# Low halves of the MLP's weights: from VectorE's subtraction to a negated copy by ScalarE and an accumulating DMA

## The chip, the cores and the metric

One core of a Trainium2 chip runs the kernel. The metric is the device time of one execution in microseconds; lower is better.

## The reference

Two layers of a hybrid decoder trunk over 512 tokens of width 1024, in float32. Each layer has a mixing part (one input projection, a gated short convolution beside chunkwise retention, one output projection) and an MLP of width 4096, each behind an RMSNorm that is modulated by a vector computed from `c`. Cut to what matters here:

```python
for l in range(DEPTH):
    mod = (c_act @ w_ada[l] + b_ada[l])[:, None, :]
    sh1, sc1, g1, sh2, sc2, g2 = jnp.split(mod, N_MOD, axis=-1)
    ...
    x = x + g1 * mix
    h2 = rms_norm(x, norm2_g[l]) * (1.0 + sc2) + sh2
    x = x + g2 * (jnp.square(jax.nn.relu(h2 @ w_up[l])) @ w_down[l])
return rms_norm(x, final_g)
```

## The kernel before

Everything is held transposed, features on partitions and the 512 tokens along the free dimension. All weights are one stream of 200 *units* of 128x1024 float32 (512 KB), 100 per layer. A unit holds eight 128x128 blocks and is the work for one bank of PSUM (or half of it, in down). There are four slots for units, `w_raw`, `w_hi` and `w_lo`, each with [4, 1024] per partition, and unit u lies in slot u % 4; four units make a *step*.

TensorE multiplies in a reduced float32 format (`F32R`), so each operand is split into a high half (the value rounded to that format) and a low half (what is left). `three` (lines 304 to 306) makes the three products high x high, high x low and low x high, so a unit is 24 matmuls. In the MLP they are 512 columns wide; a few stages around the norms are done in two halves of 256 columns.

The path of a unit in the kernel before:

- SP (`load_weight`, line 224) waits until the unit before it in the slot has been split (`w_lo_done`), and loads `w_raw` from HBM.
- ScalarE (`split_hi`, line 570) waits for the load (`w_in`) and until TensorE has finished the unit before it in the slot (`pe_unit`), and writes `w_hi` as a rounding copy.
- VectorE (`split_lo`, line 773) waits for `w_hi_done` and writes `w_lo` = `w_raw` - `w_hi`.
- TensorE (`unit`) waits for `w_lo_done` and does the 24 matmuls, then raises `pe_unit`.

`w_lo_done` is one count over all units, raised in their order; it releases TensorE and SP.

The order of work is written out by hand for each engine, in loops with semaphores. Stages of a layer, by step: v, q and k, four heads (steps up to 6), the output projection with half-width passes while the norm's statistics are made (`between` on ScalarE and VectorE), then the MLP in two halves of 2048 hidden features. Each half has *up* (16 units, one hidden tile each) and *down* (16 units, two for each of the eight output tiles). In up, each finished unit goes through four engines: ScalarE takes the relu out of PSUM to `buf_a` (line 732), GpSimd squares it into `buf_b` (line 1223), ScalarE copies the high half to `u_hi` (line 735), and VectorE subtracts for `u_lo` (line 815). `buf_a` and `buf_b` have two places each. In down, VectorE adds to `x` (`residual`, line 911), and in the second half's down ScalarE squares the new `x` and GpSimd adds the squares up (`add_square`, line 1169), once for two units.

Up's first unit-group in the first half is special (`first_step`): it goes over its four units in two half-width passes, and the second pass finishes them closely one after another, 12 half-width matmuls apart, so that the unit after them is due in slot 0 right when the fourth is finished.

VectorE also reduces the modulation's weights (`ada_pair`, line 784), 512 KB each, loaded by SP in the same queue as the units. GpSimd is otherwise idle in the MLP.

The core of a unit in the code:

```python
act.wait_ge(w_in[j], (l * STEPS + step) * 16 + 32)
act.wait_ge(pe_unit, u + 1)
nc.scalar.copy(w_hi[:, j, :], w_raw[:, j, :]).then_inc(w_hi_done, 1)
```

Of the kernel before, what the change touches and what calls it, by code (L numbers as in the profile page):

```python
# [34 lines left out]
SLOTS = 4  # L35
UNITS = 100
# [26 lines left out]

C_G1, C_G2, C_CONV, C_RET = 0, 8, 16, 28
PARAMS = 32

M_GATE1, M_SH2, M_SC2, M_GATE2 = range(2 * KT, MODS, KT)

# [2 lines left out]
ALU = mybir.AluOpType  # L71
# [4 lines left out]
def trunk(nc, xT, c_cols, weights, ada, params, bias, final_g, identity, tables, outT):  # L76
    with ExitStack() as ctx:
# [3 lines left out]
        def sem(name):  # L81
            return ctx.enter_context(nc.semaphore(name))
# [94 lines left out]
        c_exp, c_step, c_ps, c_ready = sem("c_exp"), sem("c_step"), sem("c_ps"), sem("c_ready")  # L177
        w_hi_done = sem("w_hi_done")
        w_lo_done = sem("w_lo_done")
        pe_half = sem("pe_half")  # L180
        pe_unit = sem("pe_unit")
        ada_done = sem("ada_done")
# [381 lines left out]
        def _(act):  # L564
            def split_hi(l, step, j):
# [3 lines left out]
                act.wait_ge(pe_unit, u + 1)  # L569
                nc.scalar.copy(w_hi[:, j, :], w_raw[:, j, :]).then_inc(w_hi_done, 1)  # L570

            def pe_has(l, u):
                act.wait_ge(pe_unit, l * UNITS + u + (SLOTS + 1))

# [96 lines left out]
            with act.Fori(0, DEPTH) as l:  # L671
# [55 lines left out]
                for half in range(2):  # L727

                    with act.Fori(0, 4) as i:
                        for j in range(SLOTS):  # L730
                            pe_has(l, i * 4 + (U_UP[half] + j))
                            nc.scalar.activation(buf_a[:, j % 2, :], ps[:, j, :], ACT.Relu).then_inc(evac_act, 1)  # L732
                            split_hi(l, i + (9 + 8 * half), j)
                            act.wait_ge(rsq_ready, l * 32 + i * 4 + (16 * half + j + 1))
                            nc.scalar.copy(u_hi[:, bass.ds(i * 4 + j, 1), :].rearrange("p a t -> p (a t)"),
                                           buf_b[:, j % 2, :]).then_inc(xs_hi, 1)

                    if half == 0:
                        with act.Fori(0, 4) as i:
                            for j in range(SLOTS):  # L740
                                split_hi(l, i + 13, j)

                added = l * SQ + SQ_MIX
                with act.Fori(0, 3) as i:
                    for m in range(2):
                        split_hi(l, i + 21, 2 * m)
                        act.wait_ge(evac_dve, l * ED + i * 2 + (2 + ED_DOWN[1] + m + 1))
                        act.wait_ge(ssum_added, added + i * 2 + m + 1)
                        nc.scalar.activation(buf_a[:, m, :], x[:, bass.ds(i * 2 + m, 1), :].rearrange("p a t -> p (a t)"),
                                             ACT.Square).then_inc(sq_ready, 1)  # L750
                        split_hi(l, i + 21, 2 * m + 1)

                def down_square(half, m):
                    act.wait_ge(evac_dve, l * ED + (2 + ED_DOWN[1] + 6 + half * 2 + m + 1))
# [14 lines left out]
        def _(dve):  # L769
# [83 lines left out]
            def between(l, step, xs, n, which, rest):  # L853


                def tiles(half, *ks):
                    for k in ks:
                        if k < KT:
                            product(xs, n, which, half, k)
                        if k:  # L860
                            low(xs, which, half, k - 1)
                rest(0)
                norm_scale(n, 0)
                split_lo(l, step, 0)
                tiles(0, 0, 1)
                rest(1)
                tiles(0, 2, 3, 4)
                rest(2)
                tiles(0, 5, 6)
                rest(3)  # L870
                tiles(0, 7, 8)
                dve.wait_ge(w_lo_done, l * UNITS + (step * SLOTS + 2 * SLOTS + 2))
                split_lo(l, step, 2)
                split_lo(l, step, 3)
                norm_scale(n, 1)
                tiles(1, *range(KT + 1))
# [124 lines left out]
            with dve.Fori(0, DEPTH) as l:  # L1001
# [98 lines left out]
                for half in range(2):  # L1100

                    with dve.Fori(0, 4) as i:
                        for j in range(SLOTS):
                            split_lo(l, i + (9 + 8 * half), j)
                            ub = bass.ds(i * 4 + j, 1)
                            xs_low(l, i * 4 + (XS_U[half] + j), u_lo[:, ub, :].rearrange("p a t -> p (a t)"),
                                   buf_b[:, j % 2, :], u_hi[:, ub, :].rearrange("p a t -> p (a t)"))
                            if half == 0 and j < 2:
                                ada_pair(l, i + 12, i * 2 + M_GATE2, j, later=True)
                        if half:  # L1110
                            with dve.If(l < DEPTH - 1):
                                for j in range(2):
                                    ada_pair(l, i + 20, i * 2 + KT, j, later=True)

                    if half == 0:
                        with dve.Fori(0, 4) as i:
                            for m in range(2):
                                split_lo(l, i + 13, 2 * m)
                                pe_has(l, i * 4 + (U_DOWN[0] + 2 * m + 1))
                                dve.wait_ge(mod_added, l * 24 + 24)  # L1120
                                residual(i * 2 + m, 2 + m, M_GATE2)
                                split_lo(l, i + 13, 2 * m + 1)
                            with dve.If(l < DEPTH - 1):
                                for j in range(2):
                                    ada_pair(l, i + 16, i * 2, j, later=True)
                    else:
                        with dve.Fori(0, 3) as i:
                            for m in range(2):
                                split_lo(l, i + 21, 2 * m)
                                pe_has(l, i * 4 + (U_DOWN[1] + 2 * m + 1))  # L1130
                                residual(i * 2 + m, 2 + m, M_GATE2)
                                split_lo(l, i + 21, 2 * m + 1)
                        with dve.If(l < DEPTH - 1):
                            dve.wait_ge(mod_added, l * 24 + 32)
                            norm_gain(l * 2 + 2, 0, mod[:, 1:2 * KT:2],
                                      par[:, bass.ds(below(l * PARAMS + PARAMS + C_G1, DEPTH * PARAMS, KT), KT)])

                        def down_rest(j):
                            if j % 2:
                                m = j // 2  # L1140
                                pe_has(l, U_DOWN[1] + 13 + 2 * m)
                                residual(6 + m, DOWN_BANK[1][m], M_GATE2, HALVES[1])

                        for m in range(2):
                            dve.wait_ge(pe_half, l * 6 + (SLOTS + m + 1))
                            residual(6 + m, DOWN_BANK[0][m], M_GATE2, HALVES[0])
                        with dve.If(l < DEPTH - 1):
                            between(l, 24, l * XS + XS, l * 2 + 2, 0, down_rest)
                        with dve.If(l > DEPTH - 2):
                            norm_scale(l * 2 + 2, 0)  # L1150
                            down_rest(1)
                            final(0)
                            down_rest(3)
                            norm_scale(l * 2 + 2, 1)
                            final(1)
# [3 lines left out]
        def _(pool):  # L1159
# [11 lines left out]
            def split_lo(l, step, j):  # L1171

                pool.wait_ge(w_hi_done, l * UNITS + step * SLOTS + (SLOTS + j + 1))
                nc.gpsimd.tensor_tensor(w_lo[:, j, :], w_raw[:, j, :], w_hi[:, j, :].bitcast(F32), ALU.subtract
                                        ).then_inc(w_lo_done, 1)

            pool.sem_inc(ssum_added, 2)
            pool.sem_inc(rope_done, 2)
# [7 lines left out]
            with pool.Fori(0, DEPTH) as l:  # L1186
# [31 lines left out]
                for half in range(2):  # L1218
                    with pool.Fori(0, 4) as i:
                        for j in range(SLOTS):  # L1220
                            pool.wait_ge(evac_act, l * EA + i * 4 + (EA_UP[half] + j + 1))
                            pool.wait_ge(xs_lo, l * XS + i * 4 + (XS_U[half] + j - 1))
                            nc.gpsimd.tensor_tensor(buf_b[:, j % 2, :], buf_a[:, j % 2, :], buf_a[:, j % 2, :], ALU.mult  # L1223
                                                    ).then_inc(rsq_ready, 1)

                clear_sum(l * 2 + 2)
                added = l * SQ + SQ_MIX
                with pool.Fori(0, 3) as i:
                    for m in range(2):
                        add_square(l * 2 + 2, added, i * 2 + m, m)  # L1230
                for s in range(6, SQ_MLP):
                    if s == 8:
                        with pool.If(l < DEPTH - 1):
# [89 lines left out]
```

## Time and profile before

| | |
|---|---|
| median of 3 runs | 1205.29 us (1204.19 to 1205.61) |
| span of the profiled execution | 1202.4 us; its own time was not taken apart from the runs, the median lies 2.9 us above it |
| TensorE matmul busy | 1158.5 us, 96% |
| VectorE busy | 700.7 us, 58% |
| ScalarE busy | 439.7 us, 37% |
| GpSimd busy | 274.2 us, 23% |
| DMA | 161.75 MB, 38.2% of 16 engines |

PE is TensorE's matmul side, DVE VectorE, ACT ScalarE, POOL GpSimd, SPq the queue that SP issues DMAs to. Matmuls are pipelined and their modelled spans overlap, so PE's busy share says whether it had work, not how near its peak it is. Idle time of an engine costs something only where another one waits for it.

### The profile page before, as it was taken

How to read it: one execution, taken by the hardware profiler on the slowest of the kernel's cores; microseconds unless marked ns; L12 is line 12 of the kernel's file. 1: busy time of each engine (PE TensorE's matmuls, PEld its weight loads, DVE VectorE, ACT ScalarE, POOL GpSimd, SP SyncE). 2: the span in 40 equal slices, each digit the busy share in tenths (PEclk: the TensorE clock that was granted, in tenths of full speed). 3: DMA queues.
4: the chain of work that ended last, by engine and by line, in shares of the span. 5: the costliest groups of instructions: out<-in, count | busy, mean ns of one | idle time of the engine just before them, and what ended most of it. 6: DMA issues, size and time to landing. Idle time of an engine off the chain costs nothing.

```text
span 1202.4 us, 17270 instructions
## 1 busy us (share of the span) xinstructions
PE 1158.5 (96%) x5702; PEld 978.4 (81%) x5702; DVE 700.7 (58%) x871; ACT 439.7 (37%) x620; POOL 274.2 (23%) x191
## 2 busy tenths in 40 slices
PE   2799999999999999999999999999999999999997
PEld 1688788899888888888897888889988888888886
DVE  7899877767443434443367897766764232333333
ACT  5445444335332123432243544424534212343220
POOL 4369210132110001120113940104222000112110
PEclk9899999999999999999999999999999999999998
DMA  9655434224443353343234433433353323232212
GB/s 358 259 175 179 153 108 154 101 107 160 160 141 138 105 190 125 115 147 105 87 136 158 164 140 127 138 120 123 108 192 119 105 89 103 88 105 93 98 36 72
DMA packets 46910, 161.75 MB, mean 135 GB/s; under 512 B 5520, under 2 KB 7696, under 8 KB 46736
## 3 DMA queue, kind: packets, MB, share of 16 engines
q1 hardware_dynamic: 46864, 161.13, 38.2%
q8 instruction: 29, 0.48, 0.2%
q14 instruction: 17, 0.14, 0.0%
HBM read 159.01 MB, written 2.10 MB: 134 GB/s over the span
## 4 chain that ended last, share of the span: by engine, by line
PE 80%; DVE 10%; issue 6%; POOL 2%; ACT 1%; DMA 0%; DVEq 0%; SPq 0%; ACTq 0%; POOLq 0%
PE ps L304 25%; PE ps L306 25%; PE ps L305 25%; DVE ada_raw L784 3%; DVE w_lo L773 2%; PE ps L484 1%; POOL buf_a L1202 1%; PE ps L469 1%; POOL buf_b L1203 1%; DVE arena L953 1%; PE ps L344 1%; DVE w_lo L989 1%; PE ps L345 1%; PE ps L346 1%; DVE ssum L944 0%
## 5 line engine op out<-in xcount | busy, mean ns | idle before, releaser
L773 DVE TENSOR_TENSOR w_lo<-w_raw,w_hi 128x1024 fp32r<-128x1024 f32 x193 | 259.4, 1346 | 300.8 <-ACT w_hi L570 298.7
L304 PE MATMUL ps<-h_hi,w_hi 128*128 128x512 f32 (+1 forms) x960 | 363.7, 379 | 3.4 <-issue 1.8
L306 PE MATMUL ps<-h_hi,w_lo 128*128 128x512 f32 (+1 forms) x960 | 360.9, 376 | 0.0
L305 PE MATMUL ps<-h_lo,w_hi 128*128 128x512 f32 (+1 forms) x960 | 360.7, 376 | 0.0
L570 ACT CAST w_hi<-w_raw 128x1024 fp32r<-128x1024 f32 x196 | 204.6, 1046 | 245.0 <-PE ps L306 230.7
L304 PEld LDWEIGHTS ps<-h_hi,w_hi 128*128 128x128 f32 x960 | 181.1, 189 | 37.2 <-issue 2.0
L304 PE MATMUL ps<-u_hi,w_hi 128*128 128x512 f32 (+1 forms) x576 | 211.0, 366 | 0.0
L305 PE MATMUL ps<-u_lo,w_hi 128*128 128x512 f32 (+1 forms) x576 | 210.5, 365 | 0.0
L306 PE MATMUL ps<-u_hi,w_lo 128*128 128x512 f32 (+1 forms) x576 | 210.5, 365 | 0.0
L306 PEld LDWEIGHTS ps<-h_hi,w_lo 128*128 128x128 f32 x960 | 181.0, 189 | 33.0
L305 PEld LDWEIGHTS ps<-h_lo,w_hi 128*128 128x128 f32 x960 | 181.1, 189 | 32.2
L1223 POOL TENSOR_TENSOR buf_b<-buf_a 128x512 f32<-128x512 f32 x64 | 70.6, 1103 | 450.7 <-ACT buf_a L732 447.1
L784 DVE CUSTOM_DVE_ANT_0 ada_raw<-ada_raw,c_act 128x1024 f32<-128x1024 f32 x80 | 124.4, 1568 | 2.3 <-DMA ada_raw<-ada 2.0
L305 PEld LDWEIGHTS ps<-u_lo,w_hi 128*128 128x128 f32 x576 | 108.6, 189 | 17.6
L304 PEld LDWEIGHTS ps<-u_hi,w_hi 128*128 128x128 f32 x576 | 108.6, 189 | 17.6
L306 PEld LDWEIGHTS ps<-u_hi,w_lo 128*128 128x128 f32 x576 | 108.6, 189 | 17.4
L911 DVE SCALAR_TENSOR_TENSOR x<-ps,mod,x 128x512 f32 (+2 forms) x60 | 38.5, 642 | 134.6 <-PE ps L306 134.6
L1169 POOL TENSOR_TENSOR ssum<-ssum,buf_a 128x256 f32<-128x256 f32 (+1 forms) x44 | 48.0, 1092 | 274.7 <-ACT buf_a L597 160.3
L732 ACT ACTIVATE buf_a<-ps 128x512 f32<-128x512 f32 x64 | 38.2, 597 | 160.4 <-PE ps L306 160.4
L304 PE MATMUL ps<-y_hi,w_hi 128*128 128x256 f32 (+1 forms) x192 | 61.6, 321 | 0.0
L305 PE MATMUL ps<-y_lo,w_hi 128*128 128x256 f32 (+1 forms) x192 | 61.1, 318 | 0.0
L306 PE MATMUL ps<-y_hi,w_lo 128*128 128x256 f32 (+1 forms) x192 | 61.1, 318 | 0.0
(123 smaller groups left out, 1066.7 us busy)
## 6 DMA issues: line engine op xcount, KB each, us to landing
w_raw<-weights SPq DMA_DIRECT2D x200, 512.0 KB, 3.3
ada_raw<-ada SPq DMA_DIRECT2D x80, 512.0 KB, 4.4
arena<-ada SPq DMA_DIRECT2D x16, 512.0 KB, 14.9
x<-xT SPq DMA_DIRECT2D x2, 1024.0 KB, 6.7
outT<-x SPq DMA_DIRECT2D x8, 256.0 KB, 2.3
tab<-tables SPq DMA_DIRECT2D x1, 1024.0 KB, 15.1
tab<-tables SPq DMA_DIRECT2D x1, 512.0 KB, 9.8
ident<-identity SPq DMA_DIRECT2D x1, 64.0 KB, 2.0
```

Source lines behind the costliest of these rows:

```text
L304: nc.tensor.matmul(out, wh, hi, start=first, stop=False, skip_group_check=True)
L305: nc.tensor.matmul(out, wh, lo, start=False, stop=False, skip_group_check=True)
L306: return nc.tensor.matmul(out, wl, hi, start=False, stop=last, skip_group_check=True)
L344: nc.tensor.matmul(out, hh, wh, start=start, stop=False, skip_group_check=True)
L345: nc.tensor.matmul(out, hh, wl, start=False, stop=False, skip_group_check=True)
L570: nc.scalar.copy(w_hi[:, j, :], w_raw[:, j, :]).then_inc(w_hi_done, 1)
L732: nc.scalar.activation(buf_a[:, j % 2, :], ps[:, j, :], ACT.Relu).then_inc(evac_act, 1)
L773: nc.vector.tensor_tensor(w_lo[:, j, :], w_raw[:, j, :], w_hi[:, j, :].bitcast(F32), ALU.subtract).then_inc(w_lo_done, 1)
L784: nc.vector.tensor_tensor_reduce(out=ada_raw[:, slot, :], in0=ada_raw[:, slot, :], in1=c_act[:], scale=1.0, scalar=0.0, op0=ALU.mult, op1= ...
L911: nc.vector.scalar_tensor_tensor(out=xm, in0=ps[:, bank, at], scalar=mod[:, bass.ds(m + gate_col, 1)], in1=xm, op0=ALU.mult, op1=ALU.add). ...
L1169: nc.gpsimd.tensor_tensor(ssum[:, at], ssum[:, at], buf_a[:, slot, at], ALU.add).then_inc(ssum_added, 1)
L1223: nc.gpsimd.tensor_tensor(buf_b[:, j % 2, :], buf_a[:, j % 2, :], buf_a[:, j % 2, :], ALU.mult).then_inc(rsq_ready, 1)
```

## The change

It concerns the 60 units per layer of steps 9 to 23, all that are split during up and down except those of the half-width stages. For them ScalarE follows the high half with a second pass, `split_neg`: it writes -1 times `w_raw` to `w_lo`, which rounds it as the high half is rounded, so that `w_lo` holds minus the high half. GpSimd (`sum_lo`) waits for it, issues a DMA from `w_raw` to `w_lo` that adds what it carries to what is there, waits for its landing, and raises `w_lo_done`. VectorE's `split_lo` is gone from these loops. `between` gets a wait on VectorE that keeps `w_lo_done` in order. Loads, TensorE's work and the other stages keep their code.

```diff
--- before.py
+++ after.py
@@ -63,6 +63,8 @@
 
 C_G1, C_G2, C_CONV, C_RET = 0, 8, 16, 28
 PARAMS = 32
+
+SUM_FIRST, SUM_STEPS = 9, 15
 
 M_GATE1, M_SH2, M_SC2, M_GATE2 = range(2 * KT, MODS, KT)
 
@@ -177,6 +179,9 @@
         c_exp, c_step, c_ps, c_ready = sem("c_exp"), sem("c_step"), sem("c_ps"), sem("c_ready")
         w_hi_done = sem("w_hi_done")
         w_lo_done = sem("w_lo_done")
+        w_neg_done = sem("w_neg_done")
+        w_sum_begun = sem("w_sum_begun")
+        w_lo_in = [sem(f"w_lo_in{j}") for j in range(SLOTS)]
         pe_half = sem("pe_half")
         pe_unit = sem("pe_unit")
         ada_done = sem("ada_done")
@@ -569,6 +574,11 @@
                 act.wait_ge(pe_unit, u + 1)
                 nc.scalar.copy(w_hi[:, j, :], w_raw[:, j, :]).then_inc(w_hi_done, 1)
 
+            def split_neg(l, step, j):
+
+                split_hi(l, step, j)
+                nc.scalar.activation(w_lo[:, j, :], w_raw[:, j, :], ACT.Copy, scale=-1.0).then_inc(w_neg_done, 1)
+
             def pe_has(l, u):
                 act.wait_ge(pe_unit, l * UNITS + u + (SLOTS + 1))
 
@@ -730,7 +740,7 @@
                         for j in range(SLOTS):
                             pe_has(l, i * 4 + (U_UP[half] + j))
                             nc.scalar.activation(buf_a[:, j % 2, :], ps[:, j, :], ACT.Relu).then_inc(evac_act, 1)
-                            split_hi(l, i + (9 + 8 * half), j)
+                            split_neg(l, i + (9 + 8 * half), j)
                             act.wait_ge(rsq_ready, l * 32 + i * 4 + (16 * half + j + 1))
                             nc.scalar.copy(u_hi[:, bass.ds(i * 4 + j, 1), :].rearrange("p a t -> p (a t)"),
                                            buf_b[:, j % 2, :]).then_inc(xs_hi, 1)
@@ -738,17 +748,17 @@
                     if half == 0:
                         with act.Fori(0, 4) as i:
                             for j in range(SLOTS):
-                                split_hi(l, i + 13, j)
+                                split_neg(l, i + 13, j)
 
                 added = l * SQ + SQ_MIX
                 with act.Fori(0, 3) as i:
                     for m in range(2):
-                        split_hi(l, i + 21, 2 * m)
+                        split_neg(l, i + 21, 2 * m)
                         act.wait_ge(evac_dve, l * ED + i * 2 + (2 + ED_DOWN[1] + m + 1))
                         act.wait_ge(ssum_added, added + i * 2 + m + 1)
                         nc.scalar.activation(buf_a[:, m, :], x[:, bass.ds(i * 2 + m, 1), :].rearrange("p a t -> p (a t)"),
                                              ACT.Square).then_inc(sq_ready, 1)
-                        split_hi(l, i + 21, 2 * m + 1)
+                        split_neg(l, i + 21, 2 * m + 1)
 
                 def down_square(half, m):
                     act.wait_ge(evac_dve, l * ED + (2 + ED_DOWN[1] + 6 + half * 2 + m + 1))
@@ -861,6 +871,7 @@
                             low(xs, which, half, k - 1)
                 rest(0)
                 norm_scale(n, 0)
+                dve.wait_ge(w_lo_done, l * UNITS + (step * SLOTS + 2 * SLOTS))
                 split_lo(l, step, 0)
                 tiles(0, 0, 1)
                 rest(1)
@@ -1101,7 +1112,6 @@
 
                     with dve.Fori(0, 4) as i:
                         for j in range(SLOTS):
-                            split_lo(l, i + (9 + 8 * half), j)
                             ub = bass.ds(i * 4 + j, 1)
                             xs_low(l, i * 4 + (XS_U[half] + j), u_lo[:, ub, :].rearrange("p a t -> p (a t)"),
                                    buf_b[:, j % 2, :], u_hi[:, ub, :].rearrange("p a t -> p (a t)"))
@@ -1115,21 +1125,17 @@
                     if half == 0:
                         with dve.Fori(0, 4) as i:
                             for m in range(2):
-                                split_lo(l, i + 13, 2 * m)
                                 pe_has(l, i * 4 + (U_DOWN[0] + 2 * m + 1))
                                 dve.wait_ge(mod_added, l * 24 + 24)
                                 residual(i * 2 + m, 2 + m, M_GATE2)
-                                split_lo(l, i + 13, 2 * m + 1)
                             with dve.If(l < DEPTH - 1):
                                 for j in range(2):
                                     ada_pair(l, i + 16, i * 2, j, later=True)
                     else:
                         with dve.Fori(0, 3) as i:
                             for m in range(2):
-                                split_lo(l, i + 21, 2 * m)
                                 pe_has(l, i * 4 + (U_DOWN[1] + 2 * m + 1))
                                 residual(i * 2 + m, 2 + m, M_GATE2)
-                                split_lo(l, i + 21, 2 * m + 1)
                         with dve.If(l < DEPTH - 1):
                             dve.wait_ge(mod_added, l * 24 + 32)
                             norm_gain(l * 2 + 2, 0, mod[:, 1:2 * KT:2],
@@ -1174,6 +1180,15 @@
                 nc.gpsimd.tensor_tensor(w_lo[:, j, :], w_raw[:, j, :], w_hi[:, j, :].bitcast(F32), ALU.subtract
                                         ).then_inc(w_lo_done, 1)
 
+            def sum_lo(l, step, j):
+
+                pool.wait_ge(w_lo_done, l * UNITS + (step * SLOTS + 2 * SLOTS + j))
+                pool.wait_ge(w_neg_done, l * SUM_STEPS * SLOTS + (step * SLOTS + (j + 1 - SUM_FIRST * SLOTS)))
+                pool.sem_inc(w_sum_begun, 1)
+                nc.gpsimd.dma_start(w_lo[:, j, :], w_raw[:, j, :], accum_op=ALU.add).then_inc(w_lo_in[j], 16)
+                pool.wait_ge(w_lo_in[j], l * SUM_STEPS * 16 + (step * 16 + (16 - SUM_FIRST * 16)))
+                pool.sem_inc(w_lo_done, 1)
+
             pool.sem_inc(ssum_added, 2)
             pool.sem_inc(rope_done, 2)
 
@@ -1222,12 +1237,19 @@
                             pool.wait_ge(xs_lo, l * XS + i * 4 + (XS_U[half] + j - 1))
                             nc.gpsimd.tensor_tensor(buf_b[:, j % 2, :], buf_a[:, j % 2, :], buf_a[:, j % 2, :], ALU.mult
                                                     ).then_inc(rsq_ready, 1)
+                            sum_lo(l, i + (9 + 8 * half), j)
+                    if half == 0:
+                        with pool.Fori(0, 4) as i:
+                            for j in range(SLOTS):
+                                sum_lo(l, i + 13, j)
 
                 clear_sum(l * 2 + 2)
                 added = l * SQ + SQ_MIX
                 with pool.Fori(0, 3) as i:
                     for m in range(2):
+                        sum_lo(l, i + 21, 2 * m)
                         add_square(l * 2 + 2, added, i * 2 + m, m)
+                        sum_lo(l, i + 21, 2 * m + 1)
                 for s in range(6, SQ_MLP):
                     if s == 8:
                         with pool.If(l < DEPTH - 1):
```

GpSimd's rows in the loop of up, for the first two units. Before (L1223 is the square):

```order
L1222 ISA [waits evac_act]
L1223 TENSOR_TENSOR buf_b<-buf_a 128x512 [waits xs_lo]
L1221 REGISTER_ALU
L1222 REGISTER_ALU [waits evac_act]
L1223 TENSOR_TENSOR buf_b<-buf_a 128x512 [waits xs_lo]
```

and now (L1238 is the square, L1188 the DMA of `sum_lo`):

```order
L1237 ISA [waits evac_act]
L1238 TENSOR_TENSOR buf_b<-buf_a 128x512 [waits xs_lo]
L1185 ISA
L1186 ISA [waits w_lo_done]
L1188 DMA w_lo<-w_raw 128x1024 [waits w_neg_done]
L1189 ISA
L1236 REGISTER_ALU [waits w_lo_in0]
L1237 REGISTER_ALU [waits evac_act]
```

Between two squares there now stand a DMA and the wait for its landing (`w_lo_in0`).

ScalarE's rows for one unit of up. Before (L732 relu, L570 high half of the weights, L735 high half of the hidden tile):

```order
L732 ACTIVATE buf_a<-ps 128x512 [waits pe_unit]
L568 ISA
L569 ISA [waits w_in0]
L570 CAST w_hi<-w_raw 128x1024 [waits pe_unit]
L734 ISA
L735 ISA [waits rsq_ready]
L735 COPY u_hi<-buf_b 128x512
```

and now:

```order
L742 ACTIVATE buf_a<-ps 128x512 [waits pe_unit]
L573 ISA
L574 ISA [waits w_in0]
L575 CAST w_hi<-w_raw 128x1024 [waits pe_unit]
L580 ACTIVATE w_lo<-w_raw 128x1024
L744 ISA
L745 ISA [waits rsq_ready]
L745 COPY u_hi<-buf_b 128x512
```

The negated copy, L580, stands behind the cast and ahead of the hidden tile's copy.

## Rows read from the trace of the kernel before

**Rows 1.** The page: busy time by engine, then 40 equal slices (PEclk: granted clock in tenths)

```profile
PE 1158.5 (96%) x5702; PEld 978.4 (81%) x5702; DVE 700.7 (58%) x871; ACT 439.7 (37%) x620; POOL 274.2 (23%) x191
...
PE   2799999999999999999999999999999999999997
...
POOL 4369210132110001120113940104222000112110
PEclk9899999999999999999999999999999999999998
```

**Rows 2.** Windows over the MLP of layer 0 and one of layer 1: busy us (instructions), clock, DMA share

```profile
core 0: us, PE busy (x) PEld busy (x) DVE busy (x) ACT busy (x) POOL busy (x), PEclk, DMA share, GB/s
...
286.00:370.00 84.00, 84.00 (x374) 69.59 (x373) 45.30 (x54) 33.85 (x47) 16.94 (x15) 1.00 0.46 162
370.00:455.00 85.00, 85.00 (x377) 70.38 (x376) 35.24 (x45) 18.03 (x19) 2.08 (x2) 1.00 0.41 147
...
540.00:605.00 65.00, 65.00 (x344) 56.23 (x343) 19.80 (x19) 13.97 (x17) 7.94 (x7) 1.00 0.27 89
...
1000.00:1100.00 100.00, 100.00 (x443) 82.81 (x442) 34.76 (x36) 35.76 (x49) 15.63 (x15) 1.00 0.28 95
```

**Rows 3.** The page's chain that ended last, by line: share of the span

```profile
PE ps L304 25%; PE ps L306 25%; PE ps L305 25%; DVE ada_raw L784 3%; DVE w_lo L773 2%; PE ps L484 1%; POOL buf_a L1202 1%; PE ps L469 1%; POOL buf_b L1203 1%; DVE arena L953 1%; PE ps L344 1%; DVE w_lo L989 1%; PE ps L345 1%; PE ps L346 1%; DVE ssum L944 0%
```

**Rows 4.** Groups by line: busy us, mean ns of one, idle time before and its releaser

```profile
L773 DVE TENSOR_TENSOR w_lo<-w_raw,w_hi 128x1024 fp32r<-128x1024 f32 x193 | 259.4, 1346 | 300.8 <-ACT w_hi L570 298.7
...
L570 ACT CAST w_hi<-w_raw 128x1024 fp32r<-128x1024 f32 x196 | 204.6, 1046 | 245.0 <-PE ps L306 230.7
...
L1223 POOL TENSOR_TENSOR buf_b<-buf_a 128x512 f32<-128x512 f32 x64 | 70.6, 1103 | 450.7 <-ACT buf_a L732 447.1
```

**Rows 5.** Timeline of ScalarE in down of layer 0: start us, us, engine, line

```profile
378.93 1.05 ACT L570 CAST w_hi<-w_raw 128x1024 fp32r<-128x1024 f32 x1 [4.38 <-PE ps L306]
384.37 1.05 ACT L570 CAST w_hi<-w_raw 128x1024 fp32r<-128x1024 f32 x1 [4.38 <-PE ps L306]
```

**Rows 6.** Timeline of GpSimd in the second down half of layer 0

```profile
549.56 1.29 POOL L1169 TENSOR_TENSOR ssum<-ssum,buf_a 128x512 f32<-128x512 f32 x1 [9.58 <-ACT buf_a L749]
```

**Rows 7.** Timelines at the first MLP unit of layer 0 (ACT, POOL, DVE, PE)

```profile
282.10 0.60 ACT L732 ACTIVATE buf_a<-ps 128x512 f32<-128x512 f32 x1 [3.58 <-PE ps L306]
282.60 1.04 ACT L570 CAST w_hi<-w_raw 128x1024 fp32r<-128x1024 f32 x1
...
282.92 1.04 POOL L1223 TENSOR_TENSOR buf_b<-buf_a 128x512 f32<-128x512 f32 x1 [15.98 <-ACT buf_a L732]
...
283.67 1.37 DVE L773 TENSOR_TENSOR w_lo<-w_raw,w_hi 128x1024 fp32r<-128x1024 f32 x1 [4.63 <-ACT w_hi L570]
...
286.22 0.40 PE L304 MATMUL ps<-h_hi,w_hi 128*128 128x512 f32 x1
```

**Rows 8.** Loads of weights in the MLP of layer 1: issue on SP's queue (ns), time to landing

```profile
L224 SPq DMA_DIRECT2D w_raw<-weights x56: 332/333/338, 862.1 to 1150.6; - x56
...
DMA to landing us min/median/max: 3.0/3.3/4.2
```

**Rows 9.** DMA issues in down of layer 0: KB each, median us to landing

```profile
w_raw<-weights SPq DMA_DIRECT2D x16, 512.0 KB, 5.8
```

**Rows 10.** Windows of few us around idle stretches of TensorE: columns as in rows 2

```profile
41.00:45.00 4.00, 3.10 (x7) 2.48 (x8) 3.96 (x8) 2.06 (x4) 0.00 (x0) 0.50 1.03 410
...
620.00:625.00 5.00, 4.09 (x35) 4.01 (x35) 2.39 (x4) 0.26 (x1) 0.00 (x0) 1.00 0.53 176
...
1192.00:1195.00 3.00, 0.61 (x4) 0.52 (x4) 0.56 (x3) 0.68 (x2) 0.72 (x1) 1.00 0.04 10
1195.00:1198.00 3.00, 1.10 (x2) 0.41 (x2) 1.72 (x5) 0.00 (x0) 0.00 (x0) 0.58 0.00 0
```

**Rows 11.** The chain in order of time: a 256-column matmul at a granted clock of 0.50

```profile
43.12 0.43 PE ps L346
```

## The prediction

> **What bounds the kernel now.** I read the page first. TensorE (PE) is busy 96% of the span, and its slices are full from the third on; VectorE is busy 58% of it, GpSimd 23% [rows 1]. Then the windows over the MLP (up and down), where the change lies: PE is busy in every microsecond of them, in layer 0 and in the 100 us of layer 1 that I took, at a granted clock of 1.00, with VectorE busy three to five tenths of the time and GpSimd at 17 of 84 us in up and 2 of 85 us in down [rows 2]. The chain that ended last says the same: three quarters of the span are the three matmul lines, and the line of the low halves, L773, is 2% [rows 3]. The groups say why: each low half costs VectorE 1.35 us, but the engine has idled 301 us in front of them, waiting for ScalarE's high half, and ScalarE has idled 231 us in front of that, waiting for PE [rows 4]. So nothing in the MLP waits for VectorE, and there is next to nothing to win there. The question is what the new path costs, and whether it keeps PE's pace. That pace is one unit (24 matmuls) per 5.44 us, the distance of two casts in down, each released by PE [rows 5]. A slot has four units to refill, but any serial resource that serves every unit has only 5.44 us.
>
> **The change part by part.** Per layer 32 low halves in up, 16 in the first down half and 12 in the second change: 60, or 120 in all.
>
> VectorE loses 120 subtractions of 1.35 us [rows 4], some 160 us of busy time. Worth 0: PE never waits for it in these windows [rows 2].
>
> ScalarE gets 120 more passes over a 128x1024 tile. The nearest row is the cast, 1.05 us [rows 4]. In up its work per unit grows from a relu, a cast and a copy (0.6, 1.04 and about 0.6 us, rows 7 with a copy taken like the relu) to 3.3 us, in down from 1.05 to 2.1 us, all under 5.44. Worth 0 in itself, but each low half begins 1.0 us later.
>
> The added wait of VectorE in the stage between up and mixing is met long before; ahead of the last residuals of layer 0 it asks for the last sum of step 23, while PE still has four half-width units (some 11 us) to go. Worth 0 up to a sum of about 8 us.
>
> GpSimd gets 120 sums, and here it is decided. It issues the accumulating DMA, waits until it has landed, and only then goes on. Behind that wait stand the next square (line 1223), which ScalarE's copy to u_hi waits for, the next sum, and through the low half's semaphore both PE and SP's next load. Call X the time from issue to landing on GpSimd. One unit then costs GpSimd X + 1.1 us in up (the square has 1.10 us [rows 4]), X in the first half of down, and X + 0.65 in the second (one addition of 1.29 us per two units [rows 6]). It keeps PE's pace only up to X = 4.3, 5.4 and 4.8 us.
>
> No row shows an accumulating DMA, so X is bounded. From below: a plain load of the same 512 KB lands in 3.0 us at best, 3.3 in the median [rows 8]. In a window in which each unit has one such load, the 16 DMA engines are busy 0.28 of the time [rows 2], 1.5 us per load, so 1.5 us of the 3.0 are passage and 1.5 fixed. A sum must read two operands: 1.5 + 2 x 1.5 = 4.5 us. And each sum's end releases one load, which shares the engines with the next sum: 1.5 more, 6.0 us. From above: loads issued four in a row land after 5.8 us in the median [rows 9]; taking the 4.3 us of it above the fixed part twice gives 10.1 us. The ends are thus 3.0 and 10.1. I take 6.0, since it counts the work that is certainly there, and GpSimd's own issue, for which SP needs 0.33 us [rows 8], is more likely to lengthen than to shorten it.
>
> On the second read there is a rule. By the Trainium skill, Collectives: The Full Stack, section "The bandwidth ceiling", a DMA that adds is slower because of two source reads on one ring, not because of the addition, and ran at half of a copy's rate. No trace here shows it. DMA: Bandwidth & Descriptors, "Anatomy of one DMA", gives 2.0 us plus bytes at 436 GB/s for a DMA from GpSimd, an estimate of 3.2 us for a plain one and 4.4 us with two reads; by 4.4 the whole change would cost some 10 us.
>
> With X = 6.0: in up 32 x (7.1 - 5.44) = 53 us; in the first half of down 16 x (6.0 - 5.44) = 9; in the second 12 x (6.65 - 5.44) = 15. Then the entry. The first unit of up is finished in four short pieces, so that PE wants slot 0 again at once: relu at 282.10, cast to 283.64, PE's first matmul on the new weights at 286.22 [rows 7]. Now the negative copy ends near 284.6, so PE stalls X - 1.6 = 4.4 us for that unit, 2.7 more than the 1.7 of the other units. Per layer 53 + 9 + 15 + 2.7 = 79 us; two layers 159 us. The profiled execution has a span of 1202.4 us, and the median of the runs is 1205.3, so 2.9 us lie around the span: 1202.4 + 159 + 2.9 = **1364 us**.
>
> **The rivals.**
> First, the sum is quick: X up to 4.3. Then GpSimd keeps up everywhere and only the entry is left, 2 x (X - 1.6): 2.8 us at the bound of 3.0, 5.4 us at 4.3, so 1208 to 1211 us. For it: half of a slot's cycle is still slack. Against it: it needs a second read and GpSimd's issue to cost 1.3 us together. Chance 0.13.
> Second, the sum is slow: X from 7.5 to 10.1, because the DMA engine's read, addition and write back of the destination do not overlap, or since GpSimd writes the descriptors itself. At 7.5 a layer pays 32 x 3.16 + 16 x 2.06 + 12 x 2.71 + 2.7 = 169 us, in all 1544 us; at 10.1, 1856 us. For it: four loads in a row already take 5.8. Against it: the engines have over half of their time free [rows 2]. Chance 0.22.
> Third, not slower: the sum lands before PE misses it even at the entry. That is one place, slot 0 after the first up unit, with 1.6 us of cover; with X at most 2.8 both entries together stay within 2.4 us, 1205 to 1208 us. Only a sum faster than every plain load of the MLP does this. Chance 0.04.
> Fourth, the clock. Where PE idled long, the granted clock fell: 0.50 at 41 to 45 us after the slow start, 0.58 at 1195 to 1198 us, after PE had been busy 0.61 us in 3; with 0.9 us idle in 5 it stayed at 1.00 [rows 10]. At the lower level, 1.2 GHz, a 256-column matmul takes 0.43 us of the chain [rows 11], and a unit at least 24 x 0.43 = 10.3 us, longer than GpSimd's 7.1. If half of the 120 units fell to it, they would add 60 x 3.2 = 192 us: 1556 us. The Trainium skill, TensorE: Matmul & The Clock Gate, "The HAM clock gate", has the clock fall after idleness and rise under work; by that rule gaps between units could bring this. Against it: gaps of 1.7 us in 7.1 are nearer to the row that kept 1.00. Chance 0.05.
> That the change does not do what it says is excluded only in part: the order of instructions shows the DMA and its wait in each unit, so the serial path is there.
>
> **How the numbers follow.** The forecast, X between 4.3 and 7.5, gets 0.56, and 1364 us. Its own range is 1211 to 1544 us. For the whole, 1208 us takes in the quick sum; at the top 1605 us is X = 8.0 (2 x (117 + 41 + 38 + 3) = 398 us). Left out are the third rival and the slowest sums, under 0.2. A difference of 0.2% (2.4 us) is about what measuring can tell. Of the third rival's 0.04, 0.03 go to the same and 0.01 to faster, since no wait of PE in the MLP is on VectorE; slower 0.96.
>
> **What would show it.** In the profile after: PE's idle time in the MLP is released by the low half's DMA, not by an engine; ScalarE's casts in down lie X apart, in up X + 1.1; GpSimd's squares start when a sum has landed, not when the relu ends; the DMA's time to landing is near 6 us; VectorE's share falls far, without effect; the clock stays at 1.00; the mixing stages, 45 to 270 us, are unchanged. I am wrong if the casts stay 5.44 us apart (the sum is under 4.3 us), if X itself is far from 6, or if GpSimd is idle while PE waits (the loop is another one, through SP's loads or ScalarE).

## The result, and the profile after

The changed kernel took 1388.69 us in the median (1383.46 to 1389.98, 4 runs) against 1205.04 us before: a ratio of 1.152, 95% interval 1.1506 to 1.1534. The forecast was 1364 us, with 1208 to 1605 us as its range.

The page of the changed kernel, profiled span 1388.2 us (the lines answer to [rows 1] and [rows 3]; q0 is the queue of GpSimd's DMAs, q1 that of SP's):

```profile
PE 1218.3 (88%) x5702; PEld 1007.2 (73%) x5702; DVE 543.2 (39%) x751; ACT 548.3 (39%) x740; POOL 369.8 (27%) x311
...
PE   3799999978869788878989999999787899897996
...
DVE  7899877611112101111037997766121000011002
...
PEclk6899999999989989899999999999998999998998
DMA  9474243346777777776743633422676676666662
...
q1 hardware_dynamic: 46864, 161.13, 34.4%
q0 software_dynamic: 17280, 62.92, 23.6%
...
DMA 42%; PE 30%; issue 13%; DVE 8%; POOL 3%; POOLq 2%; ACT 2%; DVEq 0%; ACTq 0%; SPq 0%
```

TensorE is busy 88% instead of 96%, VectorE 39% instead of 58%, and the last line, the chain by engine, is now 42% DMA. VectorE's relief bought nothing, as [rows 4] said: it had waited 301 us in front of that work.

The groups after, of the two matmul lines that open a product, of GpSimd's issue and square, and the sum's time from issue to landing (compare [rows 4]):

```profile
L309 PE MATMUL ps<-h_hi,w_hi 128*128 128x512 f32 (+1 forms) x960 | 376.7, 392 | 61.5 <-POOLq L1190 58.3
...
L309 PE MATMUL ps<-u_hi,w_hi 128*128 128x512 f32 (+1 forms) x576 | 224.1, 389 | 65.5 <-DVE u_lo L825 43.2
...
L1188 POOL DMA_DIRECT2D w_lo<-w_raw x120 | 103.6, 863 | 240.7 <-POOLq L1190 162.5
L1238 POOL TENSOR_TENSOR buf_b<-buf_a 128x512 f32<-128x512 f32 x64 | 65.9, 1030 | 350.4 <-DMA w_lo<-w_raw 318.4
...
w_lo<-w_raw POOLq DMA_DIRECT2D x120, 512.0 KB, 5.0
```

TensorE now idles 127 us in front of its first matmuls, where it idled 3 us in front of those on `h_hi` and not at all on `u_hi`. GpSimd's issue takes 0.86 us, SP's 0.33 [rows 8]. The landing is 5.0 us in the median, the square itself 1.03 us. The waits name the releasers; POOLq is GpSimd's queue, here the raising of `w_lo_done` after a landing:

```profile
POOL buf_b L1238 <- DMA w_lo<-w_raw: 318.4, 62, 8.6
...
PE ps L309 <- POOLq L1190: 80.5, 47, 5.2
...
PE ps L309 <- DVE u_lo L825: 43.2, 8, 9.3
```

Windows over the first up of layer 0, then over the first up, the first down and the second up of layer 1 (columns as printed; compare [rows 2]):

```profile
core 0: us, PE busy (x) PEld busy (x) DVE busy (x) ACT busy (x) POOL busy (x), PEclk, DMA share, GB/s
286.00:400.00 114.00, 83.98 (x321) 65.50 (x320) 20.60 (x36) 46.01 (x62) 28.49 (x31) 0.88 0.69 176
...
968.00:1084.00 116.00, 90.77 (x359) 71.40 (x358) 20.86 (x36) 49.98 (x66) 29.72 (x32) 0.88 0.66 167
1084.00:1185.00 101.00, 98.04 (x428) 79.72 (x427) 6.01 (x8) 32.64 (x33) 14.41 (x17) 1.00 0.69 167
1185.00:1285.00 100.00, 84.82 (x343) 65.37 (x342) 11.08 (x16) 47.69 (x63) 29.56 (x33) 0.95 0.69 167
```

In up TensorE is busy 0.74 to 0.85 of the time, in down of layer 1 nearly always. And the clock, 1.00 before, is at 0.88 in two of these windows.

GpSimd in the second up half of layer 1, where SP loads only weights (start, us, engine, line):

```profile
1185.29 0.86 POOL L1188 DMA_DIRECT2D w_lo<-w_raw  x1
1190.27 1.03 POOL L1238 TENSOR_TENSOR buf_b<-buf_a 128x512 f32<-128x512 f32 x1 [4.11 <-DMA w_lo<-w_raw]
1191.26 0.87 POOL L1188 DMA_DIRECT2D w_lo<-w_raw  x1
1196.67 1.03 POOL L1238 TENSOR_TENSOR buf_b<-buf_a 128x512 f32<-128x512 f32 x1 [4.54 <-DMA w_lo<-w_raw]
```

Over this stage two sums start 5.8 to 6.8 us apart, 6.24 in the mean: about 5 us to the landing, then the square, then the next issue at once. In down of layer 0, where SP also loads the modulation's weights:

```profile
416.72 0.85 POOL L1188 DMA_DIRECT2D w_lo<-w_raw  x1 [5.35 <-POOLq L1190]
422.87 0.85 POOL L1188 DMA_DIRECT2D w_lo<-w_raw  x1 [5.30 <-POOLq L1190]
432.65 0.86 POOL L1188 DMA_DIRECT2D w_lo<-w_raw  x1 [8.93 <-issue]
438.55 0.85 POOL L1188 DMA_DIRECT2D w_lo<-w_raw  x1 [5.05 <-POOLq L1190]
```

Here they start 5.9 to 6.2 us apart, and then once 9.8 us; in the whole stage two or three distances of 5.9 to 6.6 us are followed by one of 9.8 to 10.6. The chain shows that this is the sum's own landing (start, us):

```profile
416.72 5.28 DMA w_lo<-w_raw
...
422.87 8.58 DMA w_lo<-w_raw
...
432.65 5.03 DMA w_lo<-w_raw
```

Taking the starts of all 120 sums, the mean distance by stage is, in layer 0, 7.48 us in the first up, 7.32 in the first down, 7.04 in the second up, 6.34 in the second down; in layer 1, in the same order, it is 7.10, 6.20, 6.24 and 6.39. TensorE's pace is 5.44 [rows 5]. The stages with modulation loads are the first three of layer 0 and the first of layer 1: exactly those above 6.4.

Two idle stretches of TensorE, the entry and the turn from up to down in layer 0:

```profile
290.48 0.50 PE L309 MATMUL ps<-h_hi,w_hi 128*128 128x512 f32 x1 [3.63 <-POOLq L1190]
...
399.69 0.79 PE L309 MATMUL ps<-u_hi,w_hi 128*128 128x512 f32 x1 [9.25 <-DVE u_lo L825]
```

### The profile page after: what moved, and what is told of

Its sections match the earlier page's. It is cut to its first block, busy times and chain, and to the rows that moved or that the text cites. A ratio compares the mean times of both kernels' runs of the same rounds, so it can differ in the third digit from the quotient of the medians.

```text
span 1388.2 us, 17800 instructions
## 1 busy us (share of the span) xinstructions
PE 1218.3 (88%) x5702; PEld 1007.2 (73%) x5702; DVE 543.2 (39%) x751; ACT 548.3 (39%) x740; POOL 369.8 (27%) x311
## 3 DMA queue, kind: packets, MB, share of 16 engines
q0 software_dynamic: 17280, 62.92, 23.6%
## 4 chain that ended last, share of the span: by engine, by line
DMA 42%; PE 30%; issue 13%; DVE 8%; POOL 3%; POOLq 2%; ACT 2%; DVEq 0%; ACTq 0%; SPq 0%
DMA w_lo<-w_raw 41%; PE ps L309 9%; PE ps L311 9%; PE ps L310 9%; DVE ada_raw L794 2%; DVE w_lo L783 2%; PE ps L489 1%; POOL buf_b L1218 1%; POOL buf_a L1217 1%; POOL buf_b L1238 1%; PE ps L474 1%; ACT w_hi L575 1%; PE ps L349 0%; POOLq L1185 0%; PE ps L350 0%
## 5 line engine op out<-in xcount | busy, mean ns | idle before, releaser
L309 PE MATMUL ps<-h_hi,w_hi 128*128 128x512 f32 (+1 forms) x960 | 376.7, 392 | 61.5 <-POOLq L1190 58.3
L309 PE MATMUL ps<-u_hi,w_hi 128*128 128x512 f32 (+1 forms) x576 | 224.1, 389 | 65.5 <-DVE u_lo L825 43.2
L310 PE MATMUL ps<-u_lo,w_hi 128*128 128x512 f32 (+1 forms) x576 | 220.0, 382 | 0.0
L311 PE MATMUL ps<-u_hi,w_lo 128*128 128x512 f32 (+1 forms) x576 | 219.8, 382 | 0.0
L825 DVE TENSOR_TENSOR u_lo<-buf_b,u_hi 128x512 f32 x64 | 44.3, 693 | 404.3 <-ACT u_hi L745 404.3
L1188 POOL DMA_DIRECT2D w_lo<-w_raw x120 | 103.6, 863 | 240.7 <-POOLq L1190 162.5
L1238 POOL TENSOR_TENSOR buf_b<-buf_a 128x512 f32<-128x512 f32 x64 | 65.9, 1030 | 350.4 <-DMA w_lo<-w_raw 318.4
L745 ACT CAST u_hi<-buf_b 128x512 f32 x64 | 39.6, 619 | 268.8 <-POOL buf_b L1238 268.8
L310 PEld LDWEIGHTS ps<-u_lo,w_hi 128*128 128x128 f32 x576 | 116.5, 202 | 18.8
L580 ACT ACTIVATE w_lo<-w_raw 128x1024 fp32r<-128x1024 f32 x120 | 126.8, 1057 | 0.0
L783 DVE TENSOR_TENSOR w_lo<-w_raw,w_hi 128x1024 fp32r<-128x1024 f32 x73 | 103.3, 1421 | 27.6 <-ACT w_hi L575 26.7
```

Source lines behind the costliest of these rows:

```text
L309: nc.tensor.matmul(out, wh, hi, start=first, stop=False, skip_group_check=True)
L310: nc.tensor.matmul(out, wh, lo, start=False, stop=False, skip_group_check=True)
L311: return nc.tensor.matmul(out, wl, hi, start=False, stop=last, skip_group_check=True)
L580: nc.scalar.activation(w_lo[:, j, :], w_raw[:, j, :], ACT.Copy, scale=-1.0).then_inc(w_neg_done, 1)
L783: nc.vector.tensor_tensor(w_lo[:, j, :], w_raw[:, j, :], w_hi[:, j, :].bitcast(F32), ALU.subtract).then_inc(w_lo_done, 1)
L825: nc.vector.tensor_tensor(out, full, hi.bitcast(F32), ALU.subtract).then_inc(xs_lo, 1)
```

## The experiments

Seven kernels. The theory is that of the prediction: GpSimd's wait for the landing is served one unit at a time and is longer than TensorE's unit. Against it stand ScalarE's added pass and longer path, the DMA engines' throughput, and GpSimd's issue. The open points of size were the long landings, the second read, the load's share, the entry, and where a lag is paid.

**e2_pool_add.** The DMA and its wait are replaced, all else is kept:

```diff
-                nc.gpsimd.dma_start(w_lo[:, j, :], w_raw[:, j, :], accum_op=ALU.add).then_inc(w_lo_in[j], 16)
-                pool.wait_ge(w_lo_in[j], ...)
-                pool.sem_inc(w_lo_done, 1)
+                nc.gpsimd.tensor_tensor(w_lo[:, j, :], w_raw[:, j, :], w_lo[:, j, :].bitcast(F32), ALU.add
+                                        ).then_inc(w_lo_done, 1)
```

> Changed kernel, but GpSimd adds the raw weights itself (one 128x1024 addition) where it issued the DMA and waited. ScalarE's second pass stays. Theory (the wait for the DMA on GpSimd is the whole cost): an addition is about 2.4 us, GpSimd's unit 3.5 us in up, under TensorE's 5.44; only the entry of each layer waits, some 0.9 us twice: 1206 to 1210 us. Rival (ScalarE's second pass and the longer path from unit to low half cost a good part): 1230 us or more.

Measured: 1209.21 us, ratio 1.0041 (1.0027 to 1.0055). The group of GpSimd's addition:

```profile
L1188 POOL TENSOR_TENSOR w_lo<-w_raw,w_lo 128x1024 fp32r<-128x1024 f32 x120 | 304.9, 2541 | 152.8 <-ACT w_lo L580 152.8
```

With 2.54 us of addition GpSimd keeps the pace, although ScalarE still makes its second pass 120 times. So that pass and the order of the work cost at most these 5 us, and the DMA with its wait is the other 179 us. At each entry TensorE now waits 0.83 us.

**e4_two_in_flight.** The landing of one sum is awaited only after the next one is issued:

```diff
+            def next_lo(l, step, j, started):
+
+                begin(l, step, j)
+                if j:
+                    finish(l, step, j - 1)
+                elif started:
+                    finish(l, step - 1, SLOTS - 1)
```

(`begin` waits for the negated copy and issues, `finish` waits for the landing and raises `w_lo_done`.)

> Changed kernel, but GpSimd waits for the landing of a sum only after it has issued the next one, so two are in flight. Theory (the serial wait is the bound, the DMA engines are not): a unit has 5.44 us, in which the engines need 2.73 for the sum, 1.55 for the load and on average 0.8 for the modulation, 5.1 together, so it is hidden but for the entries of 3.6 us each and some bunching: 1212 to 1235 us. Rival (the engines' throughput is what the sums wait for): landings grow to 8 us and more and the time stays above 1290 us.

Measured: 1222.02 us, ratio 1.0148 (1.0131 to 1.0165). A window in the second up of layer 1 (columns as above), and the sums' time to landing:

```profile
1050.00:1120.00 70.00, 70.00 (x311) 57.96 (x310) 9.00 (x13) 38.26 (x53) 24.12 (x26) 1.00 0.86 194
...
DMA to landing us min/median/max: 4.5/6.5/9.8
```

TensorE has no idle time there, although the engines are busy 0.86 of it and a sum now lands after 6.5 us. It is not the DMA engines' throughput that bound the changed kernel, but that each landing was waited for before anything else was done: longer landings cost little once that wait is gone. The same 120 sums, each slower than before, cost 18 us instead of 184.

**e3_plain_dma.** Same queue, size, wait and order, but a copy without the addition:

```diff
-                nc.gpsimd.dma_start(w_lo[:, j, :], w_raw[:, j, :], accum_op=ALU.add).then_inc(w_lo_in[j], 16)
+                nc.gpsimd.dma_start(w_lo[:, j, :].bitcast(F32), w_raw[:, j, :]).then_inc(w_lo_in[j], 16)
```

> Changed kernel with a plain copy by the DMA in place of the addition (the low half is then the raw weight, the subtraction is left out); queue, size, waits and order are the same. Theory (the second read makes the sum slow: it held the 16 engines 2.73 us against 1.55 for a load): landing 4.9 - 1.2 = 3.7 us, GpSimd's unit about 5.0 us in up and 4.6 in down, so it keeps TensorE's pace except beside the modulation's loads: 1210 to 1240 us. Rival (the time is GpSimd's issue and the fixed way there and back, not the addition): landing 4.6 to 4.9 us and 1370 to 1390 us.

Measured: 1254.01 us, ratio 1.042 (1.0403 to 1.0438). The queue's line of the page, and the issue's duration and landing:

```profile
q0 software_dynamic: 17280, 62.92, 12.4%
...
L1188 POOL DMA_DIRECT2D w_lo<-w_raw x120: 530/593/722, 285.4 to 1221.0; - x120
...
DMA to landing us min/median/max: 2.8/3.4/8.3
```

By these medians the addition's price is 5.0 - 3.4 = 1.6 us of landing, a little more than expected (1.2). They mix the stages, though: in layer 1's first down and second up, without modulation loads, the copy lands after 2.8 and 2.9 us and the sum after 5.3 and 4.8, a difference of 2.5 and 1.9 us. The edit also writes to the float32 view of `w_lo`, so the copy leaves out the rounding to `F32R` as well; what is priced is the addition together with that rounding, and no run separates them. Engine time per DMA, from the queue's share: 12.4% of 1251.2 us over 120 is 1.29 us; with the addition it was 23.6% of 1388.2 us over 120, 2.73 us, 2.1 times as much. GpSimd's issue also falls, in the mean from 0.86 to 0.57 us. The time is 14 us above what I expected, since the modulation's loads stretch this DMA as well (8.3 us at most): in layer 1, sums start 5.43 and 5.44 us apart in the first down and the second up, TensorE's pace, and in the second up of layer 0 one distance in four is 9.3 to 9.6 us.

**e1_small_mod.** The modulation's loads of the MLP fetch 4 KB:

```diff
+                sp.dma_start(ada_raw[:, slot, 0:n],
+                             ada[bass.ds(below(b + FIRST_MODS, DEPTH * MODS), 1), :, 0:n].rearrange("a p n -> p (a n)")
+                             ).then_inc(ada_in[slot], 16)
```

> Changed kernel, but each of the modulation's loads that SP issues during the MLP (80 to 24: the 56 of them from step 9 on) fetches 4 KB instead of 512 KB, and VectorE's reduction of it reads the activation vector twice with a scale of 0.001, so the later modulation is not computed. Theory (these loads share the DMA engines with the sums, so that in the stages that have them some sums land after 8 to 10 us instead of 5): all stages run at the 6.2 to 6.4 us per unit of the last 28 units, 1389 - 63 = about 1326 us. Rival (the long landings come from GpSimd's side or from bursts of the weight loads alone): 1380 to 1390 us, long landings still there.

(The count in that text is wrong: 32 of the 80 loads were cut.) Measured: 1333.14 us, ratio 1.1084 (1.1057 to 1.1111). The issue and landing of its sums:

```profile
L1189 POOL DMA_DIRECT2D w_lo<-w_raw x120: 852/865/1010, 286.4 to 1298.7; - x120
...
DMA to landing us min/median/max: 4.5/5.0/6.4
```

The longest landing falls from 9.7 to 6.4 us, and the mean distance of sums is 6.16 to 6.43 us in all eight stages. The long landings are the modulation's loads; they cost 55.5 us, near the 63 estimated.

**e6_small_loads.** The weights' loads in the MLP are cut to 4 KB as well (`load_weight` with `n=8` for steps 9 to 23).

> Changed kernel with all of SP's loads in the MLP at 4 KB, the weights' too (stale weights are split and multiplied; the later modulation is left out as in e1_small_mod), so the sums have the DMA engines to themselves. Theory (the load that a landed sum releases shares the engines with the next sum, a little in up and fully in down): landing falls from 5.0 to about 4.5 us, GpSimd's unit to 5.9 us in up and 5.4 in down: 1260 to 1280 us. Rival (the load costs the full 1.5 us that the prediction added): landing 3.5 us, GpSimd's unit 4.9 in up, 1215 us. Other rival (sharing costs nothing): 1333 us, as with the small modulation loads.

Measured: 1284.53 us, ratio 1.0661 (1.0643 to 1.0679), 4 us above the range of the theory. The sum's landing (median, last column):

```profile
w_lo<-w_raw POOLq DMA_DIRECT2D x120, 512.0 KB, 4.5
```

Landing 4.5 us, GpSimd's unit mostly 5.8 us in up and 5.4 in the first down (5.9 and 5.5 in the mean), near what the theory said; both rivals are out. So the load's share is 0.3 us of landing in up and 0.8 in down, not 1.5, and with nothing beside it a sum alone still takes GpSimd past TensorE's pace in up. By the starts of the sums and the waits, the 80 us are about 32 in up, 5 in the first down, 18 in the second (6.2 us a unit), 15 at the half-width units (see below) and 8 at the entries. TensorE pays part of it at the turns from up to down, where it stands 1.3 to 6.1 us at a time for `u_lo`.

**e5_down0_only.** One part alone: `SUM_FIRST, SUM_STEPS = 13, 4`; the other stages keep VectorE's `split_lo`.

> One part alone: the kernel before, with negated copy and accumulating DMA only in the first half of down (16 sums per layer); up and the second down are VectorE's again. There GpSimd needs 6.2 us per sum against TensorE's 5.44 in layer 1, and 7.3 in layer 0, beside the modulation's loads. Theory (the lag is taken from the slack of four slots, some 8 us, and only what exceeds it is paid, at the start of the next up): layer 1 about 3 us, layer 0 about 20: 1220 to 1232 us. Rival (each sum longer than 5.44 us is paid in full): 12 + 30 us, 1245 us or more.

Measured: 1228.06 us, ratio 1.0193 (1.0176 to 1.021). From the first relu of the MLP to the last `residual` but one, layer 0 took 350.8 us against 330.4 before, layer 1 330.3 against 326.7: 20.4 and 3.6 us. In layer 1 sums were 6.2 us apart, 0.75 us too slow, sixteen times, which is 12 us of lag, and 3.6 were paid. TensorE's waits for a sum in layer 1 are 0.2, 0.3, 0.5 and 1.4 us, all at the end of the sixteen. The rest was covered by the slack of the four slots; that it could be made up afterwards fits VectorE's subtraction of 1.37 us per unit against TensorE's 5.44.

**e7_two_late_start.** Two in flight, and the first step of each MLP split by VectorE (`SUM_FIRST, SUM_STEPS = 10, 14`).

> The kernel with two sums in flight, in which moreover the first step of each layer's MLP (4 low halves) is VectorE's subtraction as before, so sums begin with the second step. Theory (of the 17.6 us that two in flight still lost, the entries, 3.65 and 4.25 us, are TensorE's wait for the first sum): 1222 - 8 = 1214 us, and no wait of TensorE for the first step. Rival (the pause only moves to the second step): 1220 to 1223 us.

Measured: 1209.73 us, ratio 1.0041 (1.0027 to 1.0055). TensorE's waits for a landing, first with two in flight, then here:

```profile
PE ps L309 <- POOLq L1192: 11.0, 4, 4.3
```

```profile
PE ps L309 <- POOLq L1202: 3.0, 2, 2.7
```

The two entries are gone, 8 us of wait, and 12 us of time. The relus of up show where it went: over layer 0's first step of the MLP the run with two in flight fell 5.6 us behind the kernel before, over layer 1's 6.9, while this run loses nothing there. With two in flight the granted clock was 0.83 and 0.66 in the 10 us around the end of the two stalls (290 to 300 and 875 to 885 us); here it was 1.00 over both entries. So a stall of about 4 us also brought a slower stretch behind it, which is where I put the missing 4 us; no run holds the clock fixed to separate the two. What stays is one wait of 2.7 us at the end of layer 0's sums (3.8 us of time over that stage), and in all 5 us over the kernel before.

## Why the prediction was right

**The mechanism held at each step.** TensorE's pace of 5.44 us, VectorE's 160 us worth nothing, ScalarE's pass hidden (e2), GpSimd the serial resource (e2, e4), slower by far more than can be mistaken. In the profile after, TensorE is released by the landing and GpSimd's squares start when a sum has landed, as the last part of the prediction asked, and the mixing stages, 45 to 270 us, are as before (TensorE busy 221.7 us in both). Two of its signs did not come: the clock did not stay at 1.00, and the landing is 5.0 us in the median, not 6. That the time is within 25 us of 1364 is largely luck: what the sum had too much in up (54 us over both layers) and what it left out for the modulation's loads (55 us) cancel, and most of the 25 us are a third term that it left out, the half-width units. (The top of the range is slightly off as well: X = 8.0 gives 1603 us, not 1605.) Term by term:

- **X = 6.0 us in up**: too long. Landing 4.85 us (in the second up of layer 1) and about 0.35 us of GpSimd's queue, so the unit was 6.24, not 7.1; 26 us per layer instead of 53. The mis-sized part is the load's share: 1.5 us in my sum, 0.3 measured in up (e6). The second read was about right: 2.73 us of engine time against the 3.0 that I took.
- **X = 6.0 us in down**: right in size, by other parts. Landing 5.3 us and 0.85 us between a landing and the next start make 6.2; 12 us instead of 9 in the first down, 11 instead of 15 in the second.
- **The modulation's loads**: left out. I took the load that each sum releases and forgot that [rows 9], which I used as a far bound, is from a stage with them, and loads land after 5.8 us there. 55 us in all (e1), as large as the error in up and opposite to it.
- **The last units of a layer**: put at nothing. The last units that wait for a sum are half passes of 2.9 us, and the sums do not shorten with them: 3 x 2.6 = 7.7 us per layer.
- **The entry**: a stall of 4.4 us forecast, 3.63 and 4.21 measured. With two in flight the two entries cost about 12 us against 8 us of wait (e7). In the changed kernel GpSimd sets the pace behind the entry, and the sum below closes with the bare waits.
- **Where a lag is paid.** I charged each stage on its own. In layer 1's first down, TensorE ran at 5.44 us per unit at full clock while GpSimd fell 0.75 us behind per unit. It lived on a lead that the sums had gained at the turn before it, where TensorE stood 3.2 and 4.1 us for `u_lo`; from the stage's last units on it waits again, 0.4 to 1.6 us per unit. Alone (e5), the same lag fits in the slots' slack but for 3.6 us. The total is the same when up follows with sums, not when it doesn't.

By the starts of the sums: in layer 1 the MLP's 60 units, from TensorE's first matmul on a summed low half to its first on the last of them, took 383.9 us against 313.3 before, and in layer 0 417.1. That is 71 and 104 us; with some 4 us for each entry and 1.5 us of lower clock at each end, the 186 us of span.

**The rivals.** The quick sum (up to 4.3 us) is out: with nothing beside it a sum takes 4.5 us. The slow one happens only beside the modulation's loads. The clock fell, which I had given a chance of 0.05: the mean over the span was 0.943 after 0.993. After an idle stretch of 9.25 us a 512-column matmul took 0.79 us (above), where 0.40 is usual [rows 7], that is the lower of its two levels. Yet it cost little in the changed kernel, since TensorE had time to spare while GpSimd set the pace; only at each layer's end, where a half-width unit took about 4.4 us instead of 2.9, does it lie on the path, 1.5 us each. Nor did every gap bring it down: from 1185 to 1260 us, with an idle stretch of 0.4 to 0.7 us in every unit, the granted clock was 1.00; from 1260 to 1285 us, which holds stretches of 3.6 and 5.4 us, it was 0.80. By the Trainium skill, TensorE: Matmul & The Clock Gate, "The HAM clock gate", the clock falls after idleness and rises under work; the trace agrees in both directions: behind the 5.35 us stretch that ends at 1280.65 us, 512-column matmuls start 0.43 us apart, and under continued work 0.23.

**The rule on the second read** (the Trainium skill, Collectives: The Full Stack, "The bandwidth ceiling") agrees with the size measured here: 1.29 and 2.73 us of engine time, 2.1 times. That the second read is the reason is not shown, since e3 leaves out the addition, the second read and the rounding together. The sum of the Trainium skill, DMA: Bandwidth & Descriptors, "Anatomy of one DMA", estimated 3.2 us for the plain DMA and, with two reads, 4.4; measured were 2.8 to 3.4, and 4.5 alone and 5.0 in the median beside the loads. The estimates were near, but not the 10 us of cost that I drew from 4.4: with sums that land after 4.5 us (e6) the kernel was still 80 us slower. My conditions had left out GpSimd's own instructions between a landing and the next operation, 0.35 us in up and 0.85 in down, so that up allows X = 4.0 and not 4.3, the first down 4.6 and not 5.4.

## What to carry to other kernels

Before moving work off an engine, ask who waits for it: 160 us of VectorE's time bought nothing here, not even where the new path kept pace (e2). A DMA that an engine issues and then waits for makes its latency that engine's busy time; compare it with the unit's time of the bound engine, with everything behind the wait added, or keep two in flight, or let the engine do the work itself: GpSimd's own addition took 2.54 us, the sum 4.5 at the least. Slack of several slots hides a lag for a while, so look for the payment in the stage behind, and count every stream that shares the DMA engines, also those in the other loop.

## What the runs showed of the hardware

- An accumulating DMA of 512 KB within SBUF took 2.73 us of the 16 engines against 1.29 for the plain copy, landed after 4.5 us alone, 4.8 (second up of layer 1) and 5.3 us (first down of layer 1) beside a load per unit, and after up to 9.7 us in the stages with modulation loads; the copy landed after 2.9 and 2.8 us in the same two stages of layer 1. GpSimd's issue of the sum took 0.86 us, of the copy 0.57. The copy's destination was the float32 view, the sum's was `F32R`.
- With the DMA engines busy 0.86 of the time, two sums in flight and a load per unit still kept TensorE's pace; landings rose to 6.5 us for the sums and from 3.3 to 4.3 for the loads.
- ScalarE's second pass in float32, written rounded, took 1.06 us, as the cast.
- TensorE's granted clock fell to its lower level for parts of up, among idle stretches of up to 9 us (0.88 in the mean of the first up of either layer), though the kernel as a whole was busy; with stretches of 0.4 to 0.7 us in every unit it stayed at 1.00 for 75 us.
